# Six gather slots instead of eight in a two-layer decoder kernel, the freed 16 KB keeping weight chunks

## The reference, cut to what matters

```python
def peer_ffn(h, w_q, sub_keys, u_tab, v_tab):
    q = (xt @ w_q).reshape(T, PEER_HEADS, 2, PEER_HALF)
    s = jnp.einsum('thpd,hpkd->thpk', q, sub_keys)
    s_top, i_top = lax.top_k(s, PEER_TOPK)
    cand = s_top[:, :, 0, :, None] + s_top[:, :, 1, None, :]
    best, pos = lax.top_k(cand, PEER_TOPK)
    gates = jax.nn.softmax(best, axis=-1)
    act = jnp.einsum('chkd,cd->chk', u_tab[ib], xb)
    act = jax.nn.gelu(act) * gb
    return jnp.einsum('chk,chkd->cd', act, v_tab[ib])
```

## Time and profile before

| | |
|---|---|
| median of 3 runs | 1578.14 us (1577.06 to 1578.72) |
| the profiled execution's own time | 1575.86 us |
| its span, first to last instruction | 1574.0 us |
| TensorE busy (matmul) | 1357.4 us, 86% |
| VectorE busy | 1005.6 us, 64% |
| ScalarE, GpSimd busy | 594.8 us, 568.2 us |
| moved by DMA | 637.58 MB, mean 405 GB/s |
| mean granted TensorE clock | 0.963 of 2.4 GHz |

### The profile page before, as it was taken

How to read it: one execution, slowest core, us unless ns; L and a number is a source line. 1 busy time by engine, 2 the same in 40 slices (tenths; PEclk the granted TensorE clock), 3 DMA queues, 4 the chain that set the end, 5 groups by cost and what they waited for, 6 DMA issues and landing times.

```text
span 1574.0 us, 13058 instructions
## 1 busy us (share of the span) xinstructions
PE 1357.4 (86%) x3288; PEld 587.2 (37%) x3288; DVE 1005.6 (64%) x2442; ACT 594.8 (38%) x1809; POOL 568.2 (36%) x516
## 2 busy tenths in 40 slices
PE   7899899888897988977989898879898887777777
PEld 3454344433343433333434343334343332222222
DVE  5686879964587864444467985444558896544454
ACT  1324354543342542332334443333334444333333
POOL 0024333543343433323444343323344453444341
PEclk9999999999998999989999899999899999999999
DMA  9469999999999999999999999999999999999996
GB/s 399 208 250 422 423 417 407 407 422 421 422 422 421 394 422 423 425 421 422 422 422 422 389 410 423 423 422 422 422 422 421 420 407 421 421 421 422 421 422 282
DMA packets 82297, 637.58 MB, mean 405 GB/s; under 512 B 9136, under 2 KB 9264, under 8 KB 10544
## 3 DMA queue, kind: packets, MB, share of 16 engines
q0 software_dynamic: 73728, 536.90, 82.4%
q1 hardware_dynamic: 7200, 93.85, 14.3%
q10 hardware_dynamic: 1296, 6.00, 0.9%
HBM read 635.67 MB, written 1.05 MB: 405 GB/s over the span
## 4 chain that ended last, share of the span: by engine, by line
DMA 39%; PE 36%; DVE 16%; ACT 4%; issue 4%; DVEq 0%; POOL 0%; SPq 0%; POOLq 0%; ACTq 0%
DMA ring<-in_peer_uv_dram,idx 38%; PE acc L575 22%; PE pp L338 10%; DVE ring L1239 7%; PE acc L338 1%; ACT diag L859 1%; PE tt L351 1%; DVE top_i L1025 1%; ACT weight L855 1%; DVE top L1021 1%; ACT L853 1%; ACT L722 1%; DVE row_f L1070 1%; ACT gelu L853 1%; PE pp L425 1%
## 5 line engine op out<-in xcount | busy, mean ns | idle before, releaser
L575 PE MATMUL acc<-ring,diag 128*128 128x512 f32 x2048 | 1003.9, 618 | 160.4 <-ACT diag L859 150.9
L1239 DVE CUSTOM_DVE_ANT_0 ring<-ring,xf 128x1024 f32<-128x1024 f32 x512 | 626.9, 1226 | 492.2 <-DMA ring<-in_peer_uv_dram,idx 480.5
L643 POOL DMA_INDIRECT ring<-in_peer_uv_dram,idx x512 | 568.0, 1109 | 982.9 <-PE acc L575 856.2
L575 PEld LDWEIGHTS acc<-ring,diag 128*128 128x128 f32 x2048 | 382.8, 196 | 705.3 <-issue 692.8
L853 ACT ACTIVATE gelu<-dots 128x1 f32<-128x1 f32 x512 | 103.5, 202 | 836.7 <-DVE dots L1239 836.4
L859 ACT ACTIVATE diag<-const,weight 128x128 f32<-128x128 f32 x512 | 205.5, 401 | 16.8
L855 ACT ACTIVATE weight<-gelu,gates 128x1 f32<-128x1 f32 x512 | 150.8, 295 | 16.6
L338 PE MATMUL pp<-wring,xT 128*128 128x512 f32 (+1 forms) x272 | 130.5, 578 | 1.2 <-ACT xT L662 1.2
L338 PE MATMUL pp<-wring,rows 128*128 128x512 f32 x192 | 99.6, 600 | 0.0
L338 PEld LDWEIGHTS pp<-wring,xT 128*128 128x128 f32 x272 | 52.0, 194 | 59.4 <-issue 56.5
L338 PE MATMUL pp<-wring,qTa 128*128 128x512 f32 x112 | 57.4, 601 | 0.0
(11 more groups left out here) (114 smaller groups left out, 636.5 us busy)
## 6 DMA issues: line engine op xcount, KB each, us to landing
wring<-in_peer_w_q_dram SPq DMA_DIRECT2D x14, 2048.0 KB, 11.9
wring<-in_conv_w_in_dram SPq DMA_DIRECT2D x12, 2048.0 KB, 12.0
wring<-in_w_qkv_dram SPq DMA_DIRECT2D x5, 2048.0 KB, 12.0
ring<-in_peer_uv_dram,idx POOLq DMA_INDIRECT x512, 15.3
wring<-in_conv_w_out_dram SPq DMA_DIRECT2D x4, 2048.0 KB, 11.7
ring<-in_w_qkv_dram SPq DMA_DIRECT2D x3, 2048.0 KB, 32.0
wring<-in_w_o_dram SPq DMA_DIRECT2D x3, 2048.0 KB, 12.6
ring<-in_w_qkv_dram SPq DMA_DIRECT2D x2, 1024.0 KB, 8.6
```

Of the source, the lines that this page charges most:

```text
L575: mm = nc.tensor.matmul(acc[half][:, :], diag[:, s % RING, :], row[:, D + half * 512:D + (half + 1) * 512], start=(k == 0), stop=(k == SLO ...
L643: nc.gpsimd.indirect_dma_start(dst, None, uv_dram, bass.IndirectOffsetOnAxis(idx[:, at:at + 1], 0)).then_inc(landed, 16)
L1239: nc.vector.tensor_tensor_reduce(row[:, 0:D], row[:, 0:D], xf[:, s // SLOTS % 2, :], 1.0, 0.0, ALU.mult, ALU.add, dots[:, s % RING:s % RIN ...
```

## The change

`RING` becomes 6. The array `ring` keeps eight rows, so its last two (place 5, 16 KB a partition) never hold a gather. Three things follow. The chunk (0, out, 0), which place 5 held before and which window 1 needs again, stays there, and its second load (1, out, 0) goes. When window 1's output projection has used it, place 5 takes (2, wq, 2), which stays for window 3, and the load of (3, wq, 2) goes. The first slots enter a ring of six: slots 2 to 5 wait for other chunks than before. `dots`, `gelu`, `weight` and `diag` have six places too.

```diff
-RING = 8
+ROWS = 8
+RING = 6
...
-        ring = sb("ring", [P, RING, 2 * D])
+        ring = sb("ring", [P, ROWS, 2 * D])
...
-        later = [what for what in later if what not in ((2, "wq", 3), (3, "wq", 3))]
+        kept = ((1, "out", 0), (2, "wq", 2), (2, "wq", 3), (3, "wq", 2), (3, "wq", 3))
+        later = [what for what in later if what not in kept]
         loads += [(*what, (i + 1) % 2) for i, what in enumerate(later)]
         loads.insert([load[:3] for load in loads].index((2, "wq", 0)), (2, "wq", 3, 6))
+        loads.insert([load[:3] for load in loads].index((2, "wq", 0)), (2, "wq", 2, 5))
...
-            if (n, what, c) == (3, "wq", 3):
+            if (n, what) == (3, "wq") and c > 1:
                 n = 2
+            if (n, what, c) == (1, "out", 0):
+                n = 0
...
                     m, was, k = previous[place]
+                    if (n, what, c) == (2, "wq", 2):
+                        m = 1
...
-                        elif ring_at(s) < 6:
+                        else:
                             written(pool, ff, (1, "in", 0))
-                        else:
-                            written(pool, pp, (0, "out", 0))
```

## The result

The changed kernel takes **1602.6 us** (median of 6 runs, 1599.51 to 1612.05), the kernel before 1576.69 on the same chip (6 runs, 1574.19 to 1578.72). The ratio is 1.0174, 95% interval 1.0146 to 1.0203, so 23 to 32 us slower. The profiled execution took 1602.28 us. The sign and the range of the prediction hold; the sum of +19.6 us was too small by about 7.

The account below looks back on a forecast made before the run. The DMA engines, at 422 GB/s from about 118 us to the end, were taken as the bound. The terms -9.9 + 24.5 + 2 + 3 = +19.6 us, laid on the median 1578.1, gave 1598 us; range 1580 to 1618.

Parts of the forecast that it names:

- Loads removed: Two 2048 KB chunks no longer loaded, 4.97 us each at 422 GB/s: -9.9 us if the DMA engines stay busy.
- The ring: Two places fewer take 5.0 us of queue away; seven stretches with short landing times lose DMA time, +24.5 us (16.0 to 35).
- the troughs' places: Seven stretches with slow consumers and short gather landing times: 228-242, 284-296, 330-348, 427-434, 505-513, 889-903, 1254-1268 us.
- 505 to 513 and 889 to 903: Two stretches, in us, with landing times of 8.0 and 8.5 us; the shorter ring should cost 5.0 and 4.5 there.
- the list: Costs of the seven short-landing stretches, each 13.0 us minus landing time, at most 5.0: 5.0, 2.8, 1.4, 2.7, 5.0, 4.5, 3.1.
- the discounts: At 284-296 and 330-348 us, 2.2 and 2.1 subtracted because the queue had only filled to 10.8 and 10.9.
- The floor of 8.0: Landing time in us a gather needs by itself; in a trough it can't fall lower, and what is missing becomes idle DMA time.
- The start: Slots 2 to 5 wait for other chunks; four gathers feed the engines for 10 us, the fifth comes late: +2 us (0 to 5).
- The loads moved: Ranking and projecting after the two old load places meet a queue not refilled, 1.5 us each: +3 us.
- Six places are enough: Rival, 8%: short landing times in troughs are still queueing, so only loads and start count: -7.9, 1570 us.
- the floor is short: Rival, 8%: a gather by itself needs only 4.5 us, so troughs cost 7.5 and the sum is -0.4: 1578 us.
- Every slot becomes slower: Rival, 12%: in window 3 a gather needs 10.9 us, pace 2.58, some 120 slots 0.1 us slower: +12 on top, 1610 us.

Follow-up runs that it names:

- loads_out: Kernel before with eight places; loads (1, out, 0) and (3, wq, 2) removed and not replaced, other chunks read instead; 1565.95 us, ratio 0.9934.
- ring6_only: Kernel before with only the ring shrunk to six places, every load as before; 1611.36 us, ratio 1.0211.
- use6: Kernel before with eight places in memory, GpSimd running only six gathers ahead; 1610.14 us, ratio 1.0212.
- use6_last: Kernel before with eight places, six in use for window 3's slots alone; 1579.19 us, ratio 1.0023.
- use6_first: Kernel before with eight places, six in use for window 0's slots alone; 1591.96 us, ratio 1.011.
- use5: Kernel before with eight places in memory, only five in use; 1709.97 us, ratio 1.0851.
- light8: Kernel before, eight places; window 1's attention does VectorE's bias, maximum and difference over 32 columns instead of 256; 1575.87 us, ratio 0.9998.
- noexp8: Kernel before, eight places; one ScalarE copy replaces the eight exponentials of window 1's attention; 1574.88 us, ratio 0.9998.
- noexp6: Kernel before with six places in use and one ScalarE copy replacing the eight exponentials of window 1's attention; 1607.01 us, ratio 1.0204.
- after_timed: Changed kernel with the old order's load gates, so no load starts earlier than before, moved load behind (2, wq, 1); 1609.14 us, ratio 1.0197.
- light6: Kernel before with six places in use and window 1's VectorE bias, maximum and difference over 32 columns; 1611.17 us, ratio 1.0223.

## Why the prediction was right, and where it was wrong

- **Loads removed, -9.9: right.** loads_out measured -10.3 (8 to 10 expected), and the changed kernel is 8.8 us below ring6_only in the medians, 11.2 in the two traces.
- **The ring, +24.5: the mis-sized term, +34 in use6.** What it rested on held: the queue in window 3 (10.3 us, 2.48 apart), the troughs' places, the trough of window 3 (3.1 foreseen, +3.15 in use6_last's medians; between slots 383 and 399 2.9 in the changed kernel, 4.1 to 4.5 in the traces of ring6_only, use6 and use6_last), and 505 to 513 and 889 to 903, foreseen at 5.0 and 4.5 (slots 127 to 143 and 255 to 279: 3.4 and 3.3 in the changed kernel, 3.5 and 4.6 in use6, 4.3 and 4.8 in ring6_only). The step that failed is in the list: "the queue had only filled to 10.8, which still owes 2.2; new 2.8" and "of which 2.1 is owed; new 1.4". These 4.2 us came out as 11.8 (10.8 in use6, 12.0 in ring6_only, 9.9 in use6_first). I had taken a queue that doesn't refill as already paid for. The sizes say that each trough pays again: use6_first, whose troughs are these and two more, measured 15.9, with 11.9 foreseen and 16.2 without the discounts. No run separates the troughs within the stretch. Without the discounts the list gives 28.8; the last 5 us of use6's 34 lie in part in the same stretch (8.5 without discounts, 10.8 measured) and for the rest in stretches that aren't on the list, such as slots 143 to 255 (2.9 us in use6).
- **The floor of 8.0: useful at six, wrong as a mechanism.** The changed kernel lands gathers in 5.5 to 7.7 us in most troughs, the shortest of its 512 in 5.5, and use5 keeps the pace at 7.8 between its late gathers, so no gather needs 8. With a floor of 5.5 the same list gives an estimate of only 13.3 us, against 34. So the rate is lost before the landing time is at its floor; that too few gathers are on the way is how I read it. The seven-place run shows that no single floor fits: at slot 47 the first place taken away cost 0.1 us, the second 5.0, the third 15.0. A floor of 8.0 would have given 2.5 each for the first two. Over the whole kernel the errors cancel: for seven the list gives 11.3 us, and 10.2 was measured. For five they don't: 7.4 us less queue make the list about 46, and with the 15 foreseen at most for window 3 about 61, where 134 was measured.
- **The start, +2: no larger than that** (1.2 to 1.7 us, not told apart from nothing). As foreseen, the fifth gather comes late. GpSimd's timeline of the changed kernel:

```profile
108.72 0.94 POOL L648 DMA_INDIRECT ring<-in_peer_uv_dram,idx  x1 [2.58 <-PE acc L343]
...
115.59 0.94 POOL L648 DMA_INDIRECT ring<-in_peer_uv_dram,idx  x1 [3.92 <-PE acc L343]
```

  These are slots 2 and 4. Four gathers stood before 115.59, where 113.4 was foreseen; the 2.2 us of the late start come on top. Those 2.2 us themselves go with a lower TensorE clock before the first gather, and not with the change. The windows view, 60 to 80 us, of the changed kernel (the granted clock is the third number from the end):

```profile
60.00:80.00 20.00, 15.73 (x43) 7.79 (x44) 9.13 (x32) 2.94 (x5) 0.00 (x0) 0.83 0.00 0
```

  and of the kernel before:

```profile
60.00:80.00 20.00, 16.76 (x48) 7.93 (x49) 8.93 (x29) 2.57 (x4) 0.00 (x0) 0.91 0.00 0
```

  The fourteen traces fall into two groups by it, whatever the number of places. Nine have 0.83 there and issue the first gather at 103.1 to 103.8 us, among them the eight-place kernels loads_out, light8 and noexp8. Five have 0.91 and issue it at 101.3 to 101.8, among them use5 and noexp6. In shorter stretches the changed kernel's clock is 0.64, 0.50 and 0.72 in 61 to 64, 64 to 67 and 67 to 70 us, after 3 us in which TensorE was busy for 1.32, and full behind them; the kernel before is at full clock there and has 0.55 in 73 to 76, after 3 us with 1.13 busy. 0.50 is the lower of the two levels, 1.2 GHz.

- **The loads moved, +3: too much; none was seen.** A load slows the slots while it runs, but the same load was only taken from a later place. What I missed is that every chunk behind comes one place earlier too; that moved time within the kernel and changed nothing that could be seen at its end.
- **The account.** In the profiled execution the spans differ by 26.5 against 19.6. The stretch of slots 47 to 79 is +7.6 against its step, the late first gather +2.2, the moved loads -3.0; the remaining steps miss by under 2 us each and add up to nearly zero.
- **The rivals.** "Six places are enough" (1570) and "the floor is short" (1578) are out: every trough lost rate. The second's price of 4.5 us was seen nowhere. The first gather, with nothing else moving when it was issued and only the second one issued behind it before it landed, took 5.5 us in the kernel before and 5.6 in the changed one; quite alone none was. The Trainium skill, DMA: Bandwidth & Descriptors, Anatomy of one DMA, gives some 4.4 us for one by itself, an estimate from its 2.0 us fixed and 436 GB/s; no run here has such a gather, and the nearest took 1.1 us more. But that price is not what decides: already a floor of 5.5 gives far too little. "Every slot becomes slower" was wrong at six and, as it was meant, at five too, where single late slots cost the time. The Trainium skill's Perfetto Trace Analysis, Identifying Performance Opportunities, says that a gap that repeats on the engine that should be saturated can mean too few buffers. This case adds that the DMA engines show no such gap in window 3 of the six-place kernel (421 GB/s), and its buffers are too few by 34 us all the same.

## What to carry to other kernels

The landing time of a prefetched transfer says how much queue there is: before a ring is cut, take (places removed) x (interval between slots) from it in every stretch. In this kernel nothing happened where enough was left (10.3 us in window 3), and where it wasn't, it is safest to let every trough pay the full amount by itself, also when the queue had no time to refill since the last one. So count troughs, not averages. As a size this held within 1 us for one place removed, was 5 us short for two, and gave less than half for three. Bytes saved were worth their full time even though the queue sometimes runs dry, but here two ring places cost 34 us and the loads bought with them gave 10.

## What had not been expected

- **How steep it is.** +10, +34 and +134 us for one, two and three gathers fewer. Every stretch shows it, not only window 3, in which five ahead also lose time to single late gathers.
- **Less queue, mostly more scatter.** The kernel before spread over 3.1 us in 16 runs (1574.12 to 1577.20) and over 5.2 at most in the other comparisons, the changed kernel over 12.5 in 6, ring6_only, use6 and after_timed over 9 to 11 in 5, use5 over 17; but light6 over 5.3 only and noexp6 over 8.2. In the changed kernel the time goes with TensorE's mean granted clock: 1599.5 us at 0.968, 1600.9 at 0.964, 1602.3 and 1602.9 at 0.963, 1607.1 at 0.957, 1612.1 at 0.958. In the 16 runs of the kernel before the clock went from 0.959 to 0.968 as well, and the time didn't follow: 1575.5 us at the lowest, 1576.7 at the highest. It would fit that the queue had hidden TensorE's pace and no longer does, and ring6_only, after_timed, noexp6 and use5 look alike. But use6 doesn't: its fastest and its slowest run, 1607.4 and 1616.8 us, both have 0.960. And light6's fastest, 1607.3, has its lowest clock, 0.958. So what scatters the time stays open; no run here varied the clock by itself.
